# Splitting 1,408 of 2,048 weight columns on GpSimd, 640 on VectorE, in the unmixed up-projection groups

## The chip, the cores and the metric

One core of one Trainium2 chip runs the whole program. The metric is device time in microseconds (us); lower is better. The kernel before was timed three times, and one further execution was profiled.

## What is computed

Two layers of a hybrid decoder trunk, for 256 prompt positions and 8 sample rows (264 columns in all, T in the kernel). Each layer is a mixer (RWKV-7, HGRN2, spatial gating) and then a PEER layer: eight heads pick 16 of 16,384 single-neuron experts for each token.

```python
def peer_ffn(h, wq, keys, down, up):
    ...
        idx = e1 * PEER_N_KEYS + e2
        gate = jax.nn.softmax(sc.astype(jnp.float32), axis=-1)
        pre = jnp.einsum("td,thkd->thk", xt, down[idx])
        act = (jax.nn.gelu(pre.astype(jnp.float32), approximate=False) * gate).astype(xt.dtype)
        return jnp.einsum("thk,thkd->td", act, up[idx])
```

The kernel does not gather experts. It multiplies by all of `down` and all of `up`, and the gates of the experts that were not picked are zero. The change is in the product with `up`.

## The kernel before

`up` is read as 128 tiles of 128 experts x 1024 columns, in groups of two (GRP = 2). A half of the tiles is 32 groups (NGRP), so a layer has 64 groups, g = 0 to 63, and two layers have 128. Of the 64 groups of a layer the first 24 (MIXED) are interleaved on TensorE with two tiles of the down projection each; the other 40 follow one another with nothing between them. In this text the former are mixed groups and the latter unmixed ones.

fp32 precision is had from fp32r operands split in a high and a low part. For the weights of group g these steps run, over two buffers b = g % 2:

- SyncE (`up`, line 399): one 1 MB DMA into the raw tiles of `ring`; it waits until both low parts of group g - 2 are made (`ulo_done`, `alo_done`).
- ScalarE (`up_hi`, line 1222): waits for the DMA and until TensorE has finished group g - 2 (`out_mm`), which read the same buffer of UHL; then copies 2048 columns into the high part of UHL, and the activations into the high part of AHL.
- GpSimd (`up_lo`, line 1906): waits for the first of these copies (`uhi_done`) and subtracts the high part from the raw weights for the second tile of the pair, 1024 columns.
- VectorE (`low`, line 1827): waits for the second copy (`ahi_done`) and does the same for the first tile, 1024 columns, then for the activations (AHL, 528 columns).
- TensorE (`up`, line 913): waits for both low parts and runs 48 matmuls, 6 for each of 8 PSUM banks; after each bank it raises `out_mm`.
- VectorE (`gather`, line 1835): adds each finished bank to xT.

VectorE's order is written out in `group`: the first four banks of g are gathered, then `low` of g + 1 runs, in some groups a multiplication by second gates (`second_gated`), then the last four banks.

```python
                def group(g, turn, p=None):

                    gather(g, range(0, 4), turn)
                    low(g + 1, turn)
                    if p is not None:
                        second_gated(p, p % 4, turn)
                    gather(g, range(4, 8), turn)
```

All VectorE tensor-by-tensor operations are recorded under the helper's line 1356, ScalarE's copies under 983 and all matmuls here under 462, so the operations are told apart by their tiles.

Of the kernel before, what the change touches and what calls it, by code (L numbers as in the profile page):

```python
# [18 lines left out]
F32 = mybir.dt.float32  # L19
U32 = mybir.dt.uint32  # L20
BF16 = mybir.dt.bfloat16
ALU = mybir.AluOpType
# [4 lines left out]
D_MODEL = 1024  # L27
# [18 lines left out]
GRP = 2  # L46
# [6 lines left out]
EXTRA = 16  # L53
AHEAD = HALF + EXTRA
MIXED = (HALF - EXTRA) // GRP


PARS = [("mix_g", 8), ("ffn_g", 8), ("mu", RT), ("w0", 4), ("a0", 4), ("kk", 4), ("ka", 4), ("rk", 4),
# [51 lines left out]
def build(nc, d):  # L110
    ctx = ExitStack()
    with ctx:
        def sb(name, *shape, dt=F32):
            return ctx.enter_context(nc.sbuf_tensor(name, list(shape), dt))
# [4 lines left out]
        ring = sb("ring", P, 2 * RINGP, KD, P)  # L119
# [131 lines left out]
        UHL = sb("UHL", P, 2, 2, GRP, D_MODEL, dt=FR)  # L251
# [32 lines left out]
        def up_bank(g, k):  # L284

            return bank[2 + k % 4] if g < MIXED else bank[k]

# [3 lines left out]
        RAWD, RAWU = 6, 0  # L291
# [12 lines left out]
        S = {n: ctx.enter_context(nc.semaphore(n)) for n in dict.fromkeys(names)}  # L304
# [40 lines left out]
        def _(sp):  # L345
# [13 lines left out]
            for l in range(DEPTH):  # L359
# [39 lines left out]
                def up(g, slot, turn):  # L399

                    sp.wait_ge(S["ulo_done"], turn + (l * 2 * NGRP + g + 1))
                    sp.wait_ge(S["alo_done"], turn + (l * 2 * NGRP + g + 1))
                    sp.dma_start(ring[:, RAWU + 2 * slot:RAWU + 2 * slot + 2].rearrange("p s k m -> p s (k m)"),
                                 d["up"][l][:, bass.ds(turn * GRP + g * GRP, GRP)]).then_inc(up_in[slot], 16)
# [12 lines left out]
                def second_gates(r, buffer, turn):  # L417

                    sp.wait_ge(S["g1_out0"], (l + 1) * (NBLK + 1) // 2 * 16)
                    sp.wait_ge(S["g1_out1"], (l + 1) * (NBLK // 2) * 16)  # L420
                    sp.wait_ge(S["g1_mul"], turn * 2 + (l * NGRP + 2 * r + 2))
                    sp.dma_start(ING[buffer], DG[:, :, bass.ds(turn * 4 + r * 4, 4)].rearrange("k p e t -> p k e t"))\
                        .then_inc(S["g1_in"], 16)

                def mixed(g, turn, more=True):

                    up(g, g % 2, turn)
                    for c in range(2 * more):
                        down(AHEAD + 2 * g + 2 + c, (2 * g + 2 + c) % 4, turn * 2, -EXTRA)

                with sp.Fori(0, MIXED // 4 - 1) as i:
                    for r in range(2):
                        mixed(2 * r, i * 4)
                        mixed(2 * r + 1, i * 4)
                        second_gates(r, r, i * 2)
                for r in range(MIXED // 2 - 2, MIXED // 2):
                    mixed(2 * r, 0)
                    mixed(2 * r + 1, 0, 2 * r + 2 < MIXED)
                    second_gates(r, r % 2, 0)
                for g in range(MIXED, NGRP + 2):  # L440
                    up(g, g % 2, 0)
                    if g in (MIXED + 2, MIXED + 4):
                        r = (g - 2) // 2
# [894 lines left out]
        def _(dve):  # L1338
# [16 lines left out]
            def tt(out, a, b, op):  # L1355
                return dve.tensor_tensor(out, a, b, op)  # L1356
# [43 lines left out]
            for l in range(DEPTH):  # L1400
# [216 lines left out]
                for lev in range(1, LEV_H + 1):  # L1617
                    hx = HV[f"HX{lev % 2}"]
                    b = 1 << (lev - 1)
# [114 lines left out]
                for tc in range(3):  # L1734
                    m, nh = (P, PH) if tc < 2 else (64, 1)
# [32 lines left out]
                for tc in (2, 0, 1):  # L1768
                    m, nh = (P, PH) if tc < 2 else (64, 1)
# [11 lines left out]
                for tc in range(3):  # L1781
                    m = P if tc < 2 else DEC
# [44 lines left out]
                def low(g, turn):  # L1827

                    b = g % 2
                    dve.wait_ge(S["ahi_done"], turn + (l * 2 * NGRP + g + 1))  # L1830
                    tt(UHL[:, b, 1, 0], ring[:, RAWU + 2 * b].rearrange("p k m -> p (k m)"),
                       UHL[:, b, 0, 0].bitcast(F32), ALU.subtract)
                    tt(AHL[:, b, 1], ACTS[:, bass.ds(turn * GRP + g % NGRP * GRP, GRP), :], AHL[:, b, 0].bitcast(F32),
                       ALU.subtract).then_inc(S["alo_done"], 1)

# [7 lines left out]
# [8 lines that stand above are left out]
                need("g_evac", GB + (l + 1) * NB)  # L1851
                low(0, 0)
                group(0, 0)
                with dve.Fori(0, MIXED // 4 - 1) as i:
# [23 lines left out]
        @block.gpsimd  # L1878
        def _(pool):

            pool.sem_inc(S["dlo_done"], 4)
            pool.sem_inc(S["ulo_done"], 2)

            for l in range(DEPTH):

                for lev in range(1, LEV_H + 1):
                    for c in range(NHC):
                        pool.wait_ge(S["att_evac"], l * 2 * (LEV_H + 1) + 2 * lev + c + 1)
                        if lev > 1:
                            pool.wait_ge(S["at_add"], l * 2 * LEV_H + 2 * (lev - 2) + c + 1)  # L1890
                        pool.tensor_tensor(AT_[:, c], AT_[:, c], (T5, T6)[c], ALU.add).then_inc(S["at_add"], 1)  # L1891

                for n in range(2, 16):
                    s = QSLOTS[n // 2]
                    pool.wait_ge(S["dhi_done"], l * ND + n - 1)
                    pool.tensor_tensor(DHL[:, n % 2, 1], ring[:, 2 * s + n % 2].rearrange("p k m -> p (k m)"),  # L1896
                                       DHL[:, n % 2, 0].bitcast(F32), ALU.subtract).then_inc(S["dlo_done"], 1)
                    if n % 2:
                        pool.drain().then_inc(ring_free[s], 1)

                def down_lo(n, b, slot, turn):
                    pool.wait_ge(S["dhi_done"], turn + (l * ND + NQ + n + 1))
                    pool.tensor_tensor(DHL[:, b, 1], ring[:, RAWD + slot].rearrange("p k e -> p (k e)"),  # L1903
                                       DHL[:, b, 0].bitcast(F32), ALU.subtract).then_inc(S["dlo_done"], 1)

                def up_lo(g, b, turn):

                    pool.wait_ge(S["uhi_done"], turn + (l * 2 * NGRP + g + 1))
                    pool.tensor_tensor(UHL[:, b, 1, 1], ring[:, RAWU + 2 * b + 1].rearrange("p k m -> p (k m)"),  # L1909
                                       UHL[:, b, 0, 1].bitcast(F32), ALU.subtract).then_inc(S["ulo_done"], 1)  # L1910

                with pool.Fori(0, AHEAD // 4) as i:
                    for b in range(4):
                        down_lo(b, b % 2, b, i * 4)
                for b in range(2):
                    down_lo(AHEAD + b, b, b, 0)

                def mixed(g, turn):

                    up_lo(g + 1, (g + 1) % 2, turn)  # L1920
                    for c in range(2):
                        down_lo(AHEAD + 2 * g + 2 + c, c, (2 * g + 2 + c) % 4, turn * 2)

                up_lo(0, 0, 0)
                with pool.Fori(0, MIXED // 2 - 1) as i:
                    for b in range(2):
                        mixed(b, i * 2)
                mixed(MIXED - 2, 0)
                for g in (MIXED, MIXED + 1):
                    up_lo(g, g % 2, 0)  # L1930
                with pool.Fori(0, NGRP - MIXED // 2 - 1) as i:
                    for b in range(2):
                        up_lo(MIXED + 2 + b, b, i * 2)
# [94 lines left out]
```

## Time and profile before

| | before |
|---|---|
| median of 3 runs | 2968.42 us (2968.40 to 2971.78) |
| profiled execution, its own time | 2967.73 us |
| span of that execution's trace | 2965.8 us |
| PE busy | 2742.1 us, 92% |
| DVE (VectorE) busy | 1888.9 us, 64% |
| ACT (ScalarE) busy | 1127.9 us, 38% |
| POOL (GpSimd) busy | 1075.9 us, 36% |
| granted TensorE clock, mean | 0.975 |

The busy shares are averages over stages that differ. PE is the matmul engine, PEld its weight load, SP the queue of SyncE. The time of the profiled execution is 1.9 us longer than its span, which begins with the first and ends with the last instruction.

### The profile page before, as it was taken

How to read it: one execution, taken by the hardware profiler on the slowest of the kernel's cores; microseconds unless marked ns; L12 is line 12 of the kernel's file. 1: busy time of each engine (PE TensorE's matmuls, PEld its weight loads, DVE VectorE, ACT ScalarE, POOL GpSimd, SP SyncE). 2: the span in 40 equal slices, each digit the busy share in tenths (PEclk: the TensorE clock that was granted, in tenths of full speed). 3: DMA queues.
4: the chain of work that ended last, by engine and by line, in shares of the span. 5: the costliest groups of instructions: out<-in, count | busy, mean ns of one | idle time of the engine just before them, and what ended most of it. 6: DMA issues, size and time to landing. Idle time of an engine off the chain costs nothing.

```text
span 2965.8 us, 55557 instructions
## 1 busy us (share of the span) xinstructions
PE 2742.1 (92%) x20766; PEld 2529.3 (85%) x20766; DVE 1888.9 (64%) x3331; ACT 1127.9 (38%) x1682; POOL 1075.9 (36%) x444
## 2 busy tenths in 40 slices
PE   7899999989987999999988999999999889999997
PEld 5687777889987999999866877778999779999997
DVE  1663562299798554689817526533995975457887
ACT  1312320344487444333303124104445864443332
POOL 0000110478843656433300001004887245663332
PEclk9999999999999999999999999999999999999998
DMA  5222223255544566455452322233555446664543
GB/s 191 101 80 82 103 75 140 88 174 175 170 146 171 199 207 205 155 194 184 143 184 72 104 72 90 88 128 129 170 170 169 152 174 206 198 199 165 195 172 107
DMA packets 145453, 439.50 MB, mean 148 GB/s; under 512 B 62066, under 2 KB 63602, under 8 KB 126772
## 3 DMA queue, kind: packets, MB, share of 16 engines
q1 hardware_dynamic: 132548, 400.84, 39.7%
q10 hardware_dynamic: 12784, 37.00, 3.3%
q8 instruction: 82, 1.34, 0.2%
q14 instruction: 39, 0.32, 0.0%
HBM read 407.10 MB, written 30.15 MB: 147 GB/s over the span
## 4 chain that ended last, share of the span: by engine, by line
PE 61%; DVE 15%; issue 12%; POOL 8%; ACT 2%; DVEq 1%; DMA 0%; POOLq 0%; ACTq 0%; SPq 0%
PE banks L462 60%; POOL DHL L1903 7%; DVE arena L1356 3%; DVE OHE L1356 2%; DVE OHG L1356 2%; DVE ACTS L1356 1%; DVE AHL L1356 1%; ACT arena L983 1%; DVE UHL L1356 1%; POOL arena L1891 1%; DVE hT L1364 1%; DVE arena L1685 0%; DVE arena L1457 0%; DVEq L1356 0%; ACT L983 0%
## 5 line engine op out<-in xcount | busy, mean ns | idle before, releaser
L462 PE MATMUL banks<-HHL,DHL 128*128 128x264 f32 x6816 | 859.4, 287 | 23.6 <-POOL DHL L1903 12.1
L462 PEld LDWEIGHTS banks<-HHL,DHL 128*128 128x128 f32 x6816 | 844.2, 190 | 32.3 <-POOL DHL L1903 16.5
L462 PE MATMUL banks<-AHL,UHL 128*128 128x264 f32 x6144 | 773.3, 286 | 31.6 <-DVE AHL L1356 29.1
L462 PEld LDWEIGHTS banks<-AHL,UHL 128*128 128x128 f32 x6144 | 758.6, 189 | 41.9 <-issue 41.8
L1903 POOL TENSOR_TENSOR DHL<-ring,DHL 128x1024 fp32r<-128x1024 f32 x256 | 657.3, 2572 | 277.8 <-ACT DHL L983 276.0
L1356 DVE TENSOR_TENSOR xT<-xT,banks 128x264 f32<-128x264 f32 x1040 | 402.7, 423 | 388.8 <-PE banks L462 387.9
L462 PE MATMUL banks<-hT,ring 128*128 128x272 f32 (+1 forms) x2048 | 501.8, 403 | 9.7 <-issue 7.9
L1909 POOL TENSOR_TENSOR UHL<-ring,UHL 128x1024 fp32r<-128x1024 f32 x128 | 308.7, 2412 | 538.2 <-ACT UHL L983 538.2
L462 PEld LDWEIGHTS banks<-hT,ring 128*128 128x128 f32 x2048 | 394.4, 196 | 101.7 <-issue 23.1
L983 ACT ACTIVATE UHL<-ring 128x2048 fp32r<-128x2048 f32 x128 | 245.5, 1918 | 509.8 <-PE banks L462 486.7
L983 ACT ACTIVATE arena<-banks 128x264 f32<-128x264 f32 (+6 forms) x226 | 98.7, 455 | 635.9 <-PE banks L462 587.2
L983 ACT ACTIVATE DHL<-ring 128x1024 fp32r<-128x1024 f32 x284 | 298.6, 1052 | 102.2 <-PE banks L462 91.8
L1891 POOL TENSOR_TENSOR arena<-arena 128x512 f32<-128x512 f32 x28 | 39.8, 1437 | 756.8 <-DVE arena L1356 756.7
L1356 DVE TENSOR_TENSOR arena<-arena 128x512 f32<-128x512 f32 (+8 forms) x222 | 207.9, 957 | 145.0 <-ACT arena L983 139.8
L462 PEld LDWEIGHTS banks<-arena 64*64 64x64 f32 (+3 forms) x3376 | 196.4, 154 | 68.6 <-DVE arena L1356 35.3
L462 PE MATMUL banks<-arena 64*64 64x64 f32 (+7 forms) x3376 | 219.3, 244 | 35.6 <-DVE arena L1356 24.0
L1356 DVE TENSOR_TENSOR UHL<-ring,UHL 128x1024 fp32r<-128x1024 f32 x128 | 236.6, 1849 | 7.5 <-ACT AHL L983 7.5
L983 ACT ACTIVATE ACTS<-banks 128x264 f32 (+1 forms) x224 | 87.8, 392 | 288.8 <-PE banks L462 281.3
L462 PE MATMUL banks<-OHG,OH 128*128 128x128 f32 x1056 | 134.0, 282 | 46.0 <-DVE ACTS L1356 40.6
L1896 POOL TENSOR_TENSOR DHL<-ring,DHL 128x1024 fp32r<-128x1024 f32 x28 | 70.0, 2504 | 287.9 <-ACT DHL L983 287.9
L462 PEld LDWEIGHTS banks<-OHG,OH 128*128 128x128 f32 x1056 | 125.6, 195 | 53.1 <-issue 38.2
L462 PE MATMUL banks<-arena,ring 128*128 128x264 f32 x640 | 149.6, 392 | 11.5 <-DVE arena L1356 8.8
(118 smaller groups left out, 1925.1 us busy)
## 6 DMA issues: line engine op xcount, KB each, us to landing
ring<-down SPq DMA_DIRECT2D x256, 512.0 KB, 3.7
ring<-up SPq DMA_DIRECT2D x128, 1024.0 KB, 4.9
ring<-wm SPq DMA_DIRECT2D x100, 1024.0 KB, 5.0
hT<-second_gates SPq DMA_DIRECT2D x32, 528.0 KB, 4.9
second_gates<-ring ACTq DMA_DIRECT2D x12, 768.0 KB, 3.3
second_gates<-hT ACTq DMA_DIRECT2D x10, 768.0 KB, 3.3
ACTS<-extra_acts SPq DMA_DIRECT2D x2, 2112.0 KB, 9.8
arena<-hs ACTq DMA_DIRECT2D x2, 1280.0 KB, 6.1
```

The costliest lines, as they stand in the source:

```text
L462: return pe.matmul(out, lhsT, rhs, start=start, stop=stop)
L983: return act.activation(out, in_, fn, **kw)
L1356: return dve.tensor_tensor(out, a, b, op)
L1364: return dve.scalar_tensor_tensor(out=out, in0=a, scalar=s, in1=b, op0=op0, op1=op1)
L1891: pool.tensor_tensor(AT_[:, c], AT_[:, c], (T5, T6)[c], ALU.add).then_inc(S["at_add"], 1)
L1896: pool.tensor_tensor(DHL[:, n % 2, 1], ring[:, 2 * s + n % 2].rearrange("p k m -> p (k m)"), DHL[:, n % 2, 0].bitcast(F32), ALU.subtract). ...
L1903: pool.tensor_tensor(DHL[:, b, 1], ring[:, RAWD + slot].rearrange("p k e -> p (k e)"), DHL[:, b, 0].bitcast(F32), ALU.subtract).then_inc(S ...
L1909: pool.tensor_tensor(UHL[:, b, 1, 1], ring[:, RAWU + 2 * b + 1].rearrange("p k m -> p (k m)"), UHL[:, b, 0, 1].bitcast(F32), ALU.subtract) ...
```

## The change

A constant SHARE = 640 is added. In the unmixed groups (g from 24 on) VectorE's subtraction covers the first 640 columns of the first tile, and GpSimd's covers the other 384 columns of it and the 1024 of the second, 1408 in all, in one instruction. In the mixed groups both sizes stay at 1024. No instruction is added, removed or put in another place, and no wait changes. On GpSimd 40 instructions of a layer grow from 128x1024 to 128x1408, on VectorE 40 shrink from 128x1024 to 128x640.

```diff
+SHARE = 640
...
                     dve.wait_ge(S["ahi_done"], turn + (l * 2 * NGRP + g + 1))
-                    tt(UHL[:, b, 1, 0], ring[:, RAWU + 2 * b].rearrange("p k m -> p (k m)"),
-                       UHL[:, b, 0, 0].bitcast(F32), ALU.subtract)
+                    own = D_MODEL if g < MIXED else SHARE
+                    tt(UHL[:, b, 1, 0, 0:own], ring[:, RAWU + 2 * b].rearrange("p k m -> p (k m)")[:, 0:own],
+                       UHL[:, b, 0, 0, 0:own].bitcast(F32), ALU.subtract)
...
                     pool.wait_ge(S["uhi_done"], turn + (l * 2 * NGRP + g + 1))
-                    pool.tensor_tensor(UHL[:, b, 1, 1], ring[:, RAWU + 2 * b + 1].rearrange("p k m -> p (k m)"),
-                                       UHL[:, b, 0, 1].bitcast(F32), ALU.subtract).then_inc(S["ulo_done"], 1)
+                    rest = slice(D_MODEL if g < MIXED else SHARE, GRP * D_MODEL)
+                    pool.tensor_tensor(UHL[:, b, 1].rearrange("p j m -> p (j m)")[:, rest],
+                                       ring[:, RAWU + 2 * b:RAWU + 2 * b + 2].rearrange("p s k m -> p (s k m)")[:, rest],
+                                       UHL[:, b, 0].rearrange("p j m -> p (j m)")[:, rest].bitcast(F32), ALU.subtract)\
+                        .then_inc(S["ulo_done"], 1)
```

## Rows read from the trace of the kernel before

**Rows 1.** The page: span, and busy time of each engine.
```profile
span 2965.8 us, 55557 instructions
...
PE 2742.1 (92%) x20766; PEld 2529.3 (85%) x20766; DVE 1888.9 (64%) x3331; ACT 1127.9 (38%) x1682; POOL 1075.9 (36%) x444
```
**Rows 2.** Windows, layer 1: mixed groups, then unmixed; PE, PEld, DVE, ACT, POOL, clock, DMA.
```profile
2450.00:2680.00 230.00, 230.00 (x1890) 230.00 (x1890) 115.72 (x214) 100.46 (x119) 143.90 (x60) 1.00 0.60 196
2700.00:2945.00 245.00, 234.51 (x1872) 229.47 (x1872) 215.35 (x401) 94.31 (x77) 91.24 (x38) 1.00 0.49 174
```
**Rows 3.** Timeline, PE, mixed groups of layer 0: start, duration, instructions.
```profile
1208.35 6.00 PE L462 MATMUL banks<-AHL,UHL 128*128 128x264 f32 x48
1214.18 6.00 PE L462 MATMUL banks<-HHL,DHL 128*128 128x264 f32 x48
```
**Rows 4.** Timeline, PE, unmixed groups of layer 1; in brackets the idle time before.
```profile
2826.49 11.96 PE L462 MATMUL banks<-AHL,UHL 128*128 128x264 f32 x96 [1.15 <-DVE AHL L1356]
2838.96 11.96 PE L462 MATMUL banks<-AHL,UHL 128*128 128x264 f32 x96 [0.51 <-DVE AHL L1356]
2851.44 0.76 PE L462 MATMUL banks<-AHL,UHL 128*128 128x264 f32 x4 [0.51 <-DVE AHL L1356]
```
**Rows 5.** Waits in the unmixed stretch of layer 1: total us, times, longest.
```profile
PE banks L462 <- DVE AHL L1356: 9.6, 20, 1.1
```
**Rows 6.** Waits in the unmixed stretch of layer 0.
```profile
PE banks L462 <- DVE AHL L1356: 10.1, 19, 1.1
```
**Rows 7.** Timeline, layer 1, two groups: what ScalarE, GpSimd and VectorE do for UHL and AHL.
```profile
2838.57 1.91 ACT L983 ACTIVATE UHL<-ring 128x2048 fp32r<-128x2048 f32 x1 [3.38 <-PE banks L462]
...
2840.56 2.41 POOL L1909 TENSOR_TENSOR UHL<-ring,UHL 128x1024 fp32r<-128x1024 f32 x1 [3.43 <-ACT UHL L983]
...
2842.55 1.50 DVE L1356 TENSOR_TENSOR UHL<-ring,UHL 128x1024 fp32r<-128x1024 f32 x1
2843.97 0.70 DVE L1356 TENSOR_TENSOR AHL<-ACTS,AHL 128x528 fp32r<-128x528 f32 x1
...
2845.21 1.92 ACT L983 ACTIVATE UHL<-ring 128x2048 fp32r<-128x2048 f32 x1 [4.20 <-PE banks L462]
...
2847.21 2.40 POOL L1909 TENSOR_TENSOR UHL<-ring,UHL 128x1024 fp32r<-128x1024 f32 x1 [4.24 <-ACT UHL L983]
...
2848.39 2.30 DVE L1356 TENSOR_TENSOR UHL<-ring,UHL 128x1024 fp32r<-128x1024 f32 x1
2850.61 0.70 DVE L1356 TENSOR_TENSOR AHL<-ACTS,AHL 128x528 fp32r<-128x528 f32 x1
```
**Rows 8.** Timeline, layer 1: the longest overlap of a DVE and a POOL subtraction.
```profile
2822.26 2.40 POOL L1909 TENSOR_TENSOR UHL<-ring,UHL 128x1024 fp32r<-128x1024 f32 x1 [5.02 <-ACT UHL L983]
...
2822.81 2.93 DVE L1356 TENSOR_TENSOR UHL<-ring,UHL 128x1024 fp32r<-128x1024 f32 x1
```
**Rows 9.** Timeline, layer 0: a pair without overlap.
```profile
1360.56 2.40 POOL L1909 TENSOR_TENSOR UHL<-ring,UHL 128x1024 fp32r<-128x1024 f32 x1 [2.85 <-ACT UHL L983]
...
1363.12 1.22 DVE L1356 TENSOR_TENSOR UHL<-ring,UHL 128x1024 fp32r<-128x1024 f32 x1
```
**Rows 10.** Lines and tiles, whole trace: min/median/max ns of one.
```profile
L1909 POOL TENSOR_TENSOR UHL<-ring,UHL x128: 2387/2397/3337, 943.1 to 2934.5; 128x1024 fp32r<-128x1024 f32 x128
...
L1891 POOL TENSOR_TENSOR arena<-arena x28: 1262/1275/1779, 355.9 to 1865.9; 128x512 f32<-128x512 f32 x28
...
L1356 DVE TENSOR_TENSOR UHL<-ring,UHL x128: 1217/1735/2931, 943.6 to 2935.7; 128x1024 fp32r<-128x1024 f32 x128
...
L1356 DVE TENSOR_TENSOR AHL<-ACTS,AHL x128: 693/696/2839, 946.5 to 2937.9; 128x528 fp32r<-128x528 f32 x128
```
**Rows 11.** The page, costliest groups: busy us, mean ns, idle before.
```profile
L1891 POOL TENSOR_TENSOR arena<-arena 128x512 f32<-128x512 f32 x28 | 39.8, 1437 | 756.8 <-DVE arena L1356 756.7
```
**Rows 12.** The page, DMA issues: KB each, median us from issue to landing.
```profile
ring<-up SPq DMA_DIRECT2D x128, 1024.0 KB, 4.9
```

## The prediction

> **What bounds the kernel now.** I read the page first, then windows over the stage that the change touches, then its waits, then the timeline of two groups.
>
> On the page PE is busy for 92% of the span, VectorE for 64%, GpSimd for 36% [rows 1]. Read as an average this says that GpSimd has room for 384 more columns and that VectorE hardly matters. The windows say more. In the mixed groups PE is busy without a gap. In the unmixed ones it is busy for 234.51 of 245 us, and VectorE for 215.35, which is 88% [rows 2]. The clock is 1.00 in both, so it plays no part.
>
> What a group costs TensorE alone is the distance of two starts in the mixed stretch: 1214.18 - 1208.35 = 5.83 us for 48 matmuls; over several starts it is 5.84, or 11.68 us for two groups [rows 3]. Unmixed, PE starts at 2838.96 and again, after 96 matmuls, at 2851.44: 12.48 us for two groups [rows 4]. So two groups lose 0.80 us, and the wait in front of them is for VectorE's AHL, 20 times in one layer and 19 in the other [rows 5, 6]. There are 40 unmixed groups in a layer, 20 pairs; 40 pairs x 0.80 = 32 us is all that can be had in this stage.
>
> The timeline says who makes AHL late [rows 7]. The buffer of UHL that TensorE read in the group started at 2838.96 is refilled in this chain:
>
> - the group starts at 2838.96 and ScalarE's copy at 2845.21: 6.25 us, the group and a hand-over;
> - GpSimd starts 2.00 us later, at 2847.21, and takes 2.40, to 2849.61;
> - VectorE's UHL subtraction, begun at 2848.39, ends at 2850.69, which is 1.08 us after GpSimd's end;
> - AHL starts at 2850.61 (0.08 before that end; neighbours overlap so in the rows) and TensorE 0.83 us after that, at 2851.44.
>
> 6.25 + 2.00 + 2.40 + 1.08 - 0.08 + 0.83 = 12.48. The chain closes on itself after two groups, since there are two buffers, and its length is exactly what two groups take. The other buffer's chain has the same links: AHL at 2843.97 plus 0.83 is 2844.80, just when TensorE's previous group is through (2838.96 + 5.84).
>
> The important link is the third. VectorE's subtraction takes 1.50 us, 2.30 us or 2.93 us for the same 1024 columns, and each time it ends 1.08 us after GpSimd's: 2840.56 + 2.41 = 2842.97 against 2844.05; 2849.61 against 2850.69 [rows 7]; 2824.66 against 2825.74 [rows 8]. Where GpSimd had ended before (1362.96) it takes 1.22 from its own start at 1363.12 [rows 9]. So it makes no headway while GpSimd's subtraction runs, and after that it needs its whole time but 0.14. GpSimd's own duration is the same 2.40 with and without overlap. **GpSimd and VectorE thus stand in series in this chain**, not side by side; the busy share of GpSimd hides that.
>
> The Trainium skill says the same of the cause (SBUF — State Buffer, Who interferes with whom): a VectorE instruction with two SBUF inputs and a GpSimd instruction that reads SBUF take one shared read interface in turns, for a whole instruction. By that rule the trace agrees, with the 1.08 us above. A reader of another page (Advanced Engine Details and Errata, Mode Summary) finds a note that names only VectorE's two-port modes as blocked; by that note these fp32 subtractions would run side by side, and the change would come out as the first rival below. The rows decide against it.
>
> **The change, part by part.**
>
> *VectorE, 384 columns fewer.* Slope between AHL at 528 columns, 693 ns, and UHL undisturbed at 1024, 1217 ns: 524 / 496 = 1.056 ns a column [rows 10], so 384 x 1.056 = 0.41 us off the link of 1.08, which becomes 0.67. In proportion to the whole instruction it would be 1217 x 384 / 1024 = 0.46. I take 0.41, since a fixed part does not shrink.
>
> *GpSimd, 384 columns more.* No subtraction of 1408 columns is in the trace. Between 512 columns (median 1275) and 1024 (2397) the slope is 2.19 ns, so +0.84 us and a duration of 3.24 [rows 10]. Lower end: with the mean of the 512-column row, 1437 [rows 11], the slope is 1.875, +0.72. Upper end: in proportion, 2397 / 1024 = 2.34, +0.90. I take 0.84, because both medians are of instructions that ran undisturbed.
>
> *The loop.* 0.84 longer and 0.41 shorter, both in series: +0.43 us, from 12.48 to 12.91 for two groups. GpSimd is slower per column by a factor of two, and moving columns to it costs the difference. Times 20 loops in each of two layers: 40 x 0.43 = **17.4 us**, unrounded. Lower end: 0.72 - 0.46 = 0.26, 10.6 us. Upper end: 0.90 - 0.41 = 0.49, 19.7 us.
>
> The skill prices a 2048-column fp32 add on GpSimd at 4497 ns (GPSIMD Engine Reference, Elementwise — side-by-side cycle accounting), 2.20 ns a column in proportion; by that the 1024 columns here would take 2.25 us where the row has 2.40. With 384 x 2.20 the sum would be 17.5 us, estimated; with the page's 3.09 us for 1408 columns set against the row's 2.40, it would be 11 us.
>
> *Parts that cost nothing.* GpSimd's `ulo_done` comes later by 0.84, at about 8.25 + 3.24 = 11.49 into the loop; TensorE waits for it, but AHL follows it by more than a microsecond, so it never is the last. The next 1 MB transfer waits for both low parts; AHL is the last of the two before and after. It lands 4.9 us after its issue [rows 12], and ScalarE wants it 6 us after it; this cover grows. VectorE's gathers after `low` are pushed as far as TensorE is. What VectorE does in the time gained is wait behind GpSimd. The first unmixed group of a layer is different: its GpSimd part is over long before, so VectorE's 0.41 is a true saving, at most 0.8 us for both layers, and probably lost in the next loop; I take 0. The mixed groups, the down projection and both mixers are untouched.
>
> Against the profiled execution, 2967.73 + 17.4 = 2985.1. The median of the runs is 0.7 above that execution, so the forecast of the median is **2985.8 us**.
>
> **Rivals.**
>
> *They run side by side after all (faster).* If VectorE's subtraction were not held, it would start 3.59 us after the group (2842.55 against 2838.96) and be over long before GpSimd; the loop would be 6.25 + 2.00 + 3.24 + about 0.15 = 11.64, just under the 11.68 that TensorE needs. All of the stage's loss would go: -32 us, 2936. The point that decides is whether VectorE ends 0.67 after GpSimd or before it. Against it stand rows 7 and 8. A partial form, in which GpSimd's longer instruction can be entered in its middle, has nothing for it. Chance 0.03.
>
> *GpSimd's extra columns are cheap (no change).* If the 384 columns cost it 0.41 us or less, the loop keeps its length, 2968. That needs 1.06 ns a column, half of any slope between its rows. Or the loop has slack that I overlooked; but the sum of its links is its period to 0.01 us. Chance 0.04.
>
> *The order of the two flips (slower than forecast).* If GpSimd starts later than 3.59 us into a group, VectorE takes its turn first and GpSimd's 3.24 us come after it: 3.59 + 0.81 + 3.24 = 7.64 against 5.84, a loss of 1.8 us for that group. It needs a ScalarE copy that is late by over a microsecond, by a transfer or by the gates' multiplication; the nearest in this stretch is GpSimd 0.55 before VectorE [rows 8]. If it happened in 5 to 10 groups, 9 to 18 us would come on top: 2995 to 3004. Against it: transfers get more time, not less. Chance 0.06.
>
> **How the numbers follow.** Forecast 0.87, no change 0.04, faster 0.03, slower still 0.06. The forecast's own range is 2979 (10.6) to 2988 (19.7). For the half-understood irregular places (a few in a layer where the wait was already longer, 1.15 us in one [rows 4]) I allow 4 us below, and up to 2994 towards the third rival: 2975 to 2994. A change of 0.2%, 5.9 us, is about what can be told from none; the forecast's whole range is above that. Faster 0.03, same 0.05, slower 0.92.
>
> **What would show it.** In the profile of the changed kernel: GpSimd's 128x1408 rows at 3.2 us (2.9 to 3.3); VectorE's 128x640 rows ending 0.67 us after GpSimd's, mostly 1.1 to 3 us long from their start, so that VectorE's busy time for UHL falls little or rises; two groups every 12.9 us on PE; the wait of PE for AHL near 20 x 0.9 us a layer instead of 9.6; mixed groups at 5.84 as before. The forecast is wrong if a 128x640 row ends before the GpSimd row beside it, if PE's last wait turns to UHL from GpSimd or to a transfer, or if the pairs come at 12.5 us or less.

## The result, and the profile after

| | before | changed |
|---|---|---|
| median | 2969.02 us (6 runs, 2962.9 to 2971.8) | 2988.49 us (6 runs, 2981.8 to 2998.3) |
| ratio to before | 1 | 1.0071, 95% interval 1.0057 to 1.0085 |
| profiled execution, its own time | 2967.73 us | 2991.29 us |

The kernel became slower by 19.5 us. The page of the changed kernel, span and busy times (they answer to [rows 1]):

```profile
span 2988.8 us, 55557 instructions
PE 2746.7 (92%) x20766; PEld 2532.6 (85%) x20766; DVE 1903.9 (64%) x3331; ACT 1128.0 (38%) x1682; POOL 1141.0 (38%) x444
```

VectorE has 40 x 2 x 384 columns less to subtract and is busy for 15 us **more**. In such rows waiting for GpSimd counts as busy. The groups by shape (whole trace; us busy, mean ns), and from the timeline of layer 1 a row of VectorE with no GpSimd row beside it:

```profile
L1912 POOL TENSOR_TENSOR UHL<-ring,UHL 128x1408 fp32r<-128x1408 f32 x80 | 258.4, 3230 | 274.3 <-ACT UHL L984 274.3
...
L1357 DVE TENSOR_TENSOR UHL<-ring,UHL 128x640 fp32r<-128x640 f32 x80 | 167.0, 2088 | 0.0
```

```profile
2706.06 0.82 DVE L1357 TENSOR_TENSOR UHL<-ring,UHL 128x640 fp32r<-128x640 f32 x1
```

GpSimd's 1408 columns take 3.23 us. VectorE's 640 columns need 0.82 us undisturbed, but the mean row is 2.09 us long: most of it is waiting. Windows of layer 1, mixed groups and then the unmixed stretch (columns as in [rows 2]):

```profile
2450.00:2680.00 230.00, 230.00 (x1891) 230.00 (x1890) 116.28 (x216) 101.80 (x120) 141.34 (x59) 1.00 0.61 206
2708.90:2968.80 259.90, 240.10 (x1920) 235.10 (x1918) 228.41 (x408) 96.57 (x79) 126.04 (x39) 1.00 0.47 170
```

Mixed groups run without a gap, as before. Timeline of PE in the unmixed groups, where [rows 4] had 12.48 us between starts:

```profile
2859.63 11.96 PE L463 MATMUL banks<-AHL,UHL 128*128 128x264 f32 x96 [0.95 <-DVE AHL L1357]
2872.54 11.96 PE L463 MATMUL banks<-AHL,UHL 128*128 128x264 f32 x96 [0.95 <-DVE AHL L1357]
2885.44 11.96 PE L463 MATMUL banks<-AHL,UHL 128*128 128x264 f32 x96 [0.94 <-DVE AHL L1357]
```

The starts are 12.90 us apart, and the gap in front, 0.51 before, is 0.95. The wait for AHL in the unmixed stretch of layer 1 (total, times, longest), against [rows 5]:

```profile
PE banks L463 <- DVE AHL L1357: 18.1, 19, 1.7
```

And the chain itself, against [rows 7]: the timeline of ScalarE, GpSimd and VectorE for UHL and AHL.

```profile
2865.88 1.92 ACT L984 ACTIVATE UHL<-ring 128x2048 fp32r<-128x2048 f32 x1 [4.63 <-PE banks L463]
...
2867.88 3.23 POOL L1912 TENSOR_TENSOR UHL<-ring,UHL 128x1408 fp32r<-128x1408 f32 x1 [3.85 <-ACT UHL L984]
...
2869.06 2.73 DVE L1357 TENSOR_TENSOR UHL<-ring,UHL 128x640 fp32r<-128x640 f32 x1
...
2871.71 0.69 DVE L1357 TENSOR_TENSOR AHL<-ACTS,AHL 128x528 fp32r<-128x528 f32 x1
```

Read link by link: the group's start at 2859.63 to ScalarE at 2865.88 is 6.25 us, then 2.00 to GpSimd, 3.23 to its end at 2871.11, 0.68 to VectorE's end at 2871.79, AHL from 2871.71, and 0.83 from there to PE at 2872.54. Only the third and fourth link differ from before: +0.83 and -0.40.

What the stage cost in all I take from the timeline, from the end of the last matmul of the down projection to the end of the last one with AHL, in both layers: before 257.72 and 257.34 us, changed 265.97 and 266.25. That is **+17.2 us**. The stage holds 41 products with `up` in each layer, since that of the last mixed group follows the last of the down projection; at 5.84 us each TensorE alone would need 2 x 239.4 = 478.9 us, so the kernel before loses 36 us here. The profiled executions differ by 23.6 us. Of the other 6.4 us, 4.8 lie ahead of this stage in layer 0, 2.2 between the two stages, -1.2 behind them and 0.6 outside the span; the change touches none of these (see the last section).

### The profile page after: what moved, and what is told of

It is laid out like the page before. It is cut to its first block, busy times and chain, and to the rows that moved or that the text cites. A ratio compares the mean times of both kernels' runs of the same rounds, so it can differ in the third digit from the quotient of the medians.

```text
span 2988.8 us, 55557 instructions
## 1 busy us (share of the span) xinstructions
PE 2746.7 (92%) x20766; PEld 2532.6 (85%) x20766; DVE 1903.9 (64%) x3331; ACT 1128.0 (38%) x1682; POOL 1141.0 (38%) x444
## 4 chain that ended last, share of the span: by engine, by line
PE 61%; DVE 14%; issue 13%; POOL 8%; ACT 2%; DVEq 1%; DMA 1%; POOLq 0%; ACTq 0%; SPq 0%
PE banks L463 60%; POOL DHL L1905 7%; DVE arena L1357 3%; DVE OHE L1357 2%; DVE OHG L1357 2%; DVE ACTS L1357 1%; DVE AHL L1357 1%; POOL arena L1893 1%; ACT arena L984 1%; DVE UHL L1357 1%; DVE arena L1686 0%; DVE arena L1458 0%; DVEq L1357 0%; DVE OH L1357 0%; DVE hT L1365 0%
## 5 line engine op out<-in xcount | busy, mean ns | idle before, releaser
L1912 POOL TENSOR_TENSOR UHL<-ring,UHL 128x1408 fp32r<-128x1408 f32 (+1 forms) x128 | 375.1, 2932 | 490.5 <-ACT UHL L984 490.5
L1357 DVE TENSOR_TENSOR UHL<-ring,UHL 128x640 fp32r<-128x640 f32 (+1 forms) x128 | 251.5, 1965 | 7.5 <-ACT AHL L984 7.5
```

The source lines that it names most:

```text
L1912: pool.tensor_tensor(UHL[:, b, 1].rearrange("p j m -> p (j m)")[:, rest], ring[:, RAWU + 2 * b:RAWU + 2 * b + 2].rearrange("p s k m -> p ( ...
```

## The experiments

Seven kernels were run, each compared with runs of the kernel before: median 2968.6 of 15 runs for VectorE's part alone, 1280, 1408 and the copy in two, 2969.4 of 17 runs for the other three. "Stage" is the sum over both layers, measured as above, good to 0.1 us; before it is 515.0 us. Line numbers differ by a few between kernels.

### VectorE's part alone

```diff
-                    rest = slice(D_MODEL if g < MIXED else SHARE, GRP * D_MODEL)
+                    rest = slice(D_MODEL, GRP * D_MODEL)
```

GpSimd is back at 1024 columns, VectorE has 640; 384 columns of the low part are made by nobody.

> VectorE's part of the change alone: 640 columns on VectorE, 1024 on GpSimd; the low parts of columns 640 to 1023 of the first tile are left out. Series theory: the two-group loop loses 0.41 us, 12.48 to 12.07 us, VectorE ends 0.67 us after GpSimd instead of 1.08, and the time falls by 40 x 0.41 = 16 us against before. Rival (VectorE only stands in GpSimd's shadow, its columns are free): no change. Rival (the two run side by side): minus 32 us.

Measured: 2955.43 us, ratio 0.9958 (0.9943 to 0.9973), 13 us faster where 16 were expected; stage 500.6, minus 14.4. The timeline has two groups in 12.08 us (GpSimd's starts at 2859.01 and 2871.09), and VectorE's 640 columns end 0.67 or 0.68 us after GpSimd:

```profile
2859.01 2.41 POOL L1912 TENSOR_TENSOR UHL<-ring,UHL 128x1024 fp32r<-128x1024 f32 x1 [3.43 <-ACT UHL L984]
...
2860.59 1.51 DVE L1357 TENSOR_TENSOR UHL<-ring,UHL 128x640 fp32r<-128x640 f32 x1
...
2865.25 2.40 POOL L1912 TENSOR_TENSOR UHL<-ring,UHL 128x1024 fp32r<-128x1024 f32 x1 [3.83 <-ACT UHL L984]
...
2866.44 1.89 DVE L1357 TENSOR_TENSOR UHL<-ring,UHL 128x640 fp32r<-128x640 f32 x1
```

VectorE's columns are on the path, both rivals fall. The other half of the change comes from the difference of the stages (532.2 in the changed kernel): 532.2 - 500.6 = 31.6 us for 384 more columns on GpSimd, where the sum had 40 x 0.84 = 33.6.

### The share turned the other way

```diff
-SHARE = 640
+SHARE = 1280
...
-                    tt(UHL[:, b, 1, 0, 0:own], ring[:, RAWU + 2 * b].rearrange("p k m -> p (k m)")[:, 0:own],
-                       UHL[:, b, 0, 0, 0:own].bitcast(F32), ALU.subtract)
+                    tt(UHL[:, b, 1].rearrange("p j m -> p (j m)")[:, 0:own],
+                       ring[:, RAWU + 2 * b:RAWU + 2 * b + 2].rearrange("p s k m -> p (s k m)")[:, 0:own],
+                       UHL[:, b, 0].rearrange("p j m -> p (j m)")[:, 0:own].bitcast(F32), ALU.subtract)
```

> The change's direction turned round: VectorE 1280 columns, GpSimd 768. Series theory: GpSimd 2.40 - 256 x 0.00219 = 1.84 us, VectorE's remainder 1.08 + 256 x 0.001056 = 1.35; the loop is 12.48 - 0.56 + 0.27 = 12.19 us, so 40 x 0.29 = 12 us faster than before. The chain of one group (3.59 to the subtraction, 1.49, then 0.75 to TensorE) is 5.83, just under 5.84. Rival (the change hurt for a reason of its form, one instruction across two tiles, not for its size): slower than before by a few us.

Measured: 2959.06 us, ratio 0.9974 (0.9962 to 0.9985); stage 506.0, minus 9.0. PE starts are 12.18 us apart:

```profile
2853.94 11.96 PE L463 MATMUL banks<-AHL,UHL 128*128 128x264 f32 x96 [0.22 <-DVE AHL L1357]
2866.12 11.96 PE L463 MATMUL banks<-AHL,UHL 128*128 128x264 f32 x96 [0.22 <-DVE AHL L1357]
```

The form, one instruction over two tiles, does not hurt on VectorE: the time falls. On GpSimd it is settled further down, where each of two instructions stays within one tile and the stage is as long as in the changed kernel.

The same with SHARE = 1408:

> VectorE 1408 columns, GpSimd 640: the mirror of the change. Series theory: GpSimd 1.56 us, remainder 1.49, loop 12.48 - 0.84 + 0.41 = 12.05 us; the chain of one group over VectorE alone is 3.59 + 1.62 + 0.75 = 5.96, or 11.93 for two, just below. 40 x 0.43 = 17 us faster than before. Rival (VectorE's own chain binds more than its rows say): no faster than with 1280 columns.

Measured: 2955.57 us, ratio 0.9956 (0.9940 to 0.9972); stage 501.5, minus 13.5. GpSimd's starts are 12.05 us apart, as worked out:

```profile
2858.44 1.57 POOL L1913 TENSOR_TENSOR UHL<-ring,UHL 128x640 fp32r<-128x640 f32 x1 [4.55 <-ACT UHL L984]
...
2870.49 1.56 POOL L1913 TENSOR_TENSOR UHL<-ring,UHL 128x640 fp32r<-128x640 f32 x1 [4.57 <-ACT UHL L984]
```

In the regular loop the two steps of this size mirror each other, +0.42 and -0.43 us. Over the stage 384 columns one way cost 17.2 us and the other way gave 13.5; where the rest went is said in the section on the prediction.

And with SHARE = 1536:

> VectorE 1536 columns, GpSimd 512. The two-buffer loop would be 12.48 + 512 x (0.001056 - 0.00219) = 11.90 us, but VectorE's chain within one group is now 3.59 + 1.76 + 0.75 = 6.10 us, 12.20 for two, and binds. Theory: slower than with 1408 columns, 12.20 against 12.05 us, 40 x 0.15 = 6 us; about 11 us faster than before. Rival (only the loop over GpSimd counts): 23 us faster than before.

Measured: 2956.89 us, ratio 0.9955 (0.9939 to 0.9971); stage 504.0, minus 11.0. The rival's 23 us did not come. In the regular groups VectorE no longer meets GpSimd, and its own period is the bound (timeline):

```profile
2862.34 1.29 POOL L1913 TENSOR_TENSOR UHL<-ring,UHL 128x512 fp32r<-128x512 f32 x1 [4.76 <-ACT UHL L984]
...
2863.78 1.75 DVE L1357 TENSOR_TENSOR UHL<-ring,UHL 128x1536 fp32r<-128x1536 f32 x1
...
2869.85 1.75 DVE L1357 TENSOR_TENSOR UHL<-ring,UHL 128x1536 fp32r<-128x1536 f32 x1
```

One group takes 2869.85 - 2863.78 = 6.07 us, where 6.10 was expected. The stage says that 1536 is 2.5 us worse than 1408; the medians, 1.3 us apart and measured on two chips, do not tell them apart. So the turn is near 1408, but these runs do not fix it.

### ScalarE's copy in two, GpSimd's columns first

```diff
-                    f(UHL[:, b, 0].rearrange("p a m -> p (a m)"),
-                      ring[:, RAWU + 2 * b:RAWU + 2 * b + 2].rearrange("p s k m -> p (s k m)"), ACT.Copy)\
-                        .then_inc(S["uhi_done"], 1)
+                    cut = 0 if g < MIXED else min(SHARE, D_MODEL)
+                    raw = ring[:, RAWU + 2 * b:RAWU + 2 * b + 2].rearrange("p s k m -> p (s k m)")
+                    hi = UHL[:, b, 0].rearrange("p a m -> p (a m)")
+                    f(hi[:, cut:], raw[:, cut:], ACT.Copy).then_inc(S["uhi_done"], 1)
+                    if cut:
+                        f(hi[:, 0:cut], raw[:, 0:cut], ACT.Copy)
```

With SHARE = 1024, the sizes of before:

> Shares as before (1024 and 1024), but in the unmixed groups ScalarE's copy of 2048 columns is two copies of 1024, GpSimd's tile first, so that GpSimd starts after 1.05 us instead of 1.92. Loop theory: the link of 2.00 becomes about 1.13 and the loop 11.61 us, under the 11.68 that TensorE needs; nearly the whole loss goes, minus 30 us, about 2938. Rival (the wait is set by VectorE's and GpSimd's work, not by when GpSimd starts): no change. Rival (transfer next in line: it lands just before ScalarE asks): part of the gain stays out, and ScalarE's wait for it grows.

Measured: **2939.09 us**, ratio 0.9912 (0.9895 to 0.9928), 29.5 us faster than before; stage 489.2, minus 25.8. The timeline: GpSimd starts 1.14 us after ScalarE instead of 2.00,

```profile
2864.47 2.01 ACT L984 ACTIVATE UHL<-ring 128x1024 fp32r<-128x1024 f32 x2 [3.29 <-PE banks L463]
2865.61 2.42 POOL L1915 TENSOR_TENSOR UHL<-ring,UHL 128x1024 fp32r<-128x1024 f32 x1 [3.44 <-ACT UHL L984]
...
2867.68 1.44 DVE L1360 TENSOR_TENSOR UHL<-ring,UHL 128x1024 fp32r<-128x1024 f32 x1
```

and PE runs 912 matmuls, 19 groups, without a gap:

```profile
2790.22 11.96 PE L463 MATMUL banks<-AHL,UHL 128*128 128x264 f32 x96 [0.26 <-DVE AHL L1360]
2804.05 113.00 PE L463 MATMUL banks<-AHL,UHL 128*128 128x264 f32 x912 [1.86 <-DVE AHL L1360]
```

GpSimd's subtraction is as long as before, and VectorE's ends 1.09 us after it, as before; its rows are shorter only by waiting. The point at which GpSimd may start moved, and 25.8 of the 36 us that the stage loses went: it is the loop that binds, until TensorE does. The regular groups now come at 11.71 us for two, next to TensorE's 11.68. What stays are four or five waits in a layer. The one of 1.86 us is behind a transfer: issued at 2791.26, just after one of second gates, it landed at 2798.50, 7.24 us later, and ScalarE's copy began at 2798.68. It has a second price. After this wait 14 matmuls come 0.22 us apart instead of 0.12, with a granted clock of 0.56 from 2804.05 to 2807.50, where 1.2 GHz was granted for most of the window. The group took 7.48 us, 1.6 more than its 5.84. No other wait in the unmixed groups of the nine profiles was followed by such a stretch, not even one of 2.49 us in the last experiment below.

The same with the change's shares, 640 and 1408:

> The change's shares (640 and 1408) with ScalarE's copy split in the unmixed groups: GpSimd's 1408 columns first, VectorE's 640 second. Loop theory: the first copy takes about 1.38 us instead of 1.92, so the link of 2.00 becomes 1.46 and the loop of the changed kernel, 12.90, becomes 12.36 us: 40 x 0.54 = 22 us off the changed kernel, about 2967, 5 us under before and some 27 above the split with equal shares. Rival (the split alone does the work, the share no longer matters once it is there): as fast as the split with 1024 and 1024, 2939.

Measured: 2965.62 us, ratio 0.9993 (0.9983 to 1.0003); stage 511.6. PE starts are 12.37 us apart (12.36 expected):

```profile
2835.81 11.96 PE L463 MATMUL banks<-AHL,UHL 128*128 128x264 f32 x96 [0.41 <-DVE AHL L1360]
2848.18 11.96 PE L463 MATMUL banks<-AHL,UHL 128*128 128x264 f32 x96 [0.41 <-DVE AHL L1360]
```

Against the changed kernel the stage is 20.6 us shorter, against the split with equal shares 22.4 us longer, where 27 were expected. The share still has its price while the loop is longer than TensorE's 11.68 us.

### GpSimd's 1408 columns in two instructions

```diff
+                    for part in (slice(D_MODEL, 2 * D_MODEL), slice(SHARE, D_MODEL))[0:1 if g < MIXED else 2]:
+                        ins = pool.tensor_tensor(UHL[:, b, 1].rearrange("p j m -> p (j m)")[:, part],
...
+                    ins.then_inc(S["ulo_done"], 1)
```

> The change's shares, but GpSimd's 1408 columns are two instructions, 1024 and then 384. Theory (turns are taken by whole instructions): VectorE's subtraction, already waiting, goes in between and ends about 0.68 us after the first GpSimd row, not after the second; the second then stands before or beside AHL. It costs 0.15 us more of fixed time; the loop is 12.9 to 13.1 us, so as slow as the changed kernel or a few us slower. Rival (GpSimd keeps its turn as long as it has work): VectorE ends 0.68 after the second row, and the loop is 13.05 us, plus 6.

Measured: 2984.70 us, ratio 1.0058 (1.0042 to 1.0075); stage 533.3, 1.1 more than the changed kernel. This excess is one place of layer 0, where a copy waited for a transfer and PE then waited 2.49 us; elsewhere the stage is about 1 us shorter. The timeline shows the turns; the row of 3.96 us holds both GpSimd instructions, the last row is the second of them alone.

```profile
2862.21 3.96 POOL L1913 TENSOR_TENSOR UHL<-ring,UHL 128x1024 fp32r<-128x1024 f32 x2 [3.68 <-ACT UHL L984]
...
2863.52 1.77 DVE L1357 TENSOR_TENSOR UHL<-ring,UHL 128x640 fp32r<-128x640 f32 x1
2865.22 1.52 DVE L1357 TENSOR_TENSOR AHL<-ACTS,AHL 128x528 fp32r<-128x528 f32 x1
```

```profile
2864.57 1.60 POOL L1913 TENSOR_TENSOR UHL<-ring,UHL 128x384 fp32r<-128x384 f32 x1
```

GpSimd's second row starts at 2864.57, about where the first ends. VectorE, waiting since 2863.52, goes in between and ends at 2865.29, 0.7 us after that. GpSimd's 384 columns now wait and end at 2866.17, 0.88 us after VectorE's end. VectorE's AHL, issued at 2865.22, waits for them in turn and ends at 2866.74, 0.57 us after theirs; alone it takes 0.69. So a turn is one instruction, whoever waits gets the next, and cutting the work into more turns does not shorten the sum. These rows show the turns; what the two engines share is not tested by a run.

## Why the prediction was right

Forecast 2985.8 us, measured 2988.5, +19.5 against a forecast +17.4.

*What bounds.* The loop of two groups over ScalarE, GpSimd, VectorE and TensorE, 12.48 us, against 11.68 that TensorE needs. The copy in two showed it directly: with one link shortened by 0.86 us the loop fell to 11.71 us, and of some 20 gaps on PE in a layer four or five were left. With 1408 and 1280 columns on VectorE the period came out as 12.05 and 12.18 us where the links sum to 12.05 and 12.19.

*GpSimd, +0.84 us, duration 3.24.* Measured 3.23. The slope from the 512-column row held up to 1408 columns; the upper end, in proportion, would have been 3.30, the lower 3.12.

*VectorE, -0.41 us, remainder 0.67.* Measured 0.68, and alone 12.08 us a loop for 12.07.

*The loop, 12.91 us, +17.4 us.* Measured 12.90, and the stage +17.2. The count of 40 loops is right for the regular groups only. VectorE's part alone gave 14.4 us of the stage where 40 loops have 16.4, 1280 columns 9.0 for 11.6, and 1408 columns 13.5 for 17. The start of each group, compared with the kernel before, shows where the rest is: every regular loop has nearly its full amount, and it is the first groups of a layer and the two places where ScalarE's copy waits for a transfer or the second gates that give less, or at times more. Around the second of these, in layer 1, VectorE's part alone lost 0.20 us in a loop instead of gaining 0.41, and 1408 columns lost 0.64. That the change comes so near to its sum is partly luck: 20 loops are 8.6 us, layer 0 has 8.3 and layer 1 8.9.

*Parts at nothing.* The mixed groups stayed at full speed. The first unmixed group behaved as said: TensorE began it 0.40 us earlier, and the next loop took that back, +0.83 instead of +0.43. `ulo_done` did not become the last wait; the wait in front of PE is AHL in 19 cases of a layer, 16.9 and 18.1 us, and one of 1.67 us at the start is put down to a gather. Transfers held ScalarE's copy in five groups, against three before, so their cover did not grow everywhere.

*The rivals.* Side by side: refuted by the rows, and by the two GpSimd instructions, between which VectorE waits its turn. Cheap extra columns: no, 2.16 us per thousand. The flip of order did not occur in the unmixed groups; where both were at work GpSimd came 0.48 us or more ahead of VectorE even at the irregular places. What it does to GpSimd can be read at the first groups of a layer, here layer 0 of the kernel before; the row of GpSimd holds two instructions, of which the second begins at 945.41:

```profile
943.07 5.68 POOL L1909 TENSOR_TENSOR UHL<-ring,UHL 128x1024 fp32r<-128x1024 f32 x2 [21.30 <-ACT UHL L983]
...
943.63 2.92 DVE L1356 TENSOR_TENSOR UHL<-ring,UHL 128x1024 fp32r<-128x1024 f32 x1 [3.73 <-ACT AHL L983]
```

VectorE's row ends at 946.55. GpSimd's second one ends at 948.75, 2.20 us after that, and is 3.34 us long, the maximum in [rows 10]. The prediction passes over it where it calls GpSimd's duration the same with and without overlap: GpSimd waits too, when it comes second.

*What the sum did not have.* About 2 us of the median, and 6.4 us of the profiled pair, lie outside the stage. The last section is on that. The interval of the ratio, 16.9 to 25.2 us, holds the 17.2 us of the stage, so nothing more has to be explained by the change.

## What to carry to other kernels

Where two engines take turns, an instruction each, their times add on the path, so splitting work between them gains nothing by overlap; each column should go to whichever is faster per column until that engine's own chain binds. Engines with 36% or 64% busy shares can both be critical: follow one buffer around until it returns, sum the links, and compare with what the bounding engine needs. Then look for the cheapest link to shorten; here that was not the subtraction but the point at which GpSimd was allowed to begin, and a copy cut in two gave 25.8 us of the stage where the best share gave 13.5.

## What the runs showed that I had not expected

The spread between executions of one kernel, up to 16 us, is as large as the effects. In three profiles the code ahead of the unmixed groups is the same, yet the last down projection of layer 0 ends at 1220.2 us before, at 1225.0 in the changed kernel and at 1217.2 with 1408 columns on VectorE. Windows from 300 to 400 us (columns as in [rows 2]; the clock is the third number from the right), first the kernel before, then the changed one, then 1408 columns:

```profile
300.00:400.00 100.00, 91.64 (x531) 77.21 (x529) 57.31 (x79) 34.33 (x68) 19.82 (x14) 0.92 0.26 90
```

```profile
300.00:400.00 100.00, 94.22 (x507) 79.31 (x507) 55.77 (x76) 34.49 (x67) 17.52 (x12) 0.86 0.26 90
```

```profile
300.00:400.00 100.00, 91.36 (x561) 78.22 (x561) 58.73 (x81) 36.09 (x71) 19.85 (x14) 0.98 0.26 90
```

The granted clock in this stretch of the first mixer, where TensorE is busy for 91 to 94 of 100 us, was 0.92, 0.86 and 0.98 of full speed, and the matmuls done in it 531, 507 and 561. The order of the three is that of the stage's start. The other six profiles do not keep it: VectorE's part alone had 0.95 here and ended the last down projection of layer 0 at 1224.0, the copy in two had 0.98 and ended it at 1220.4. Over the first 900 us the order holds better: the three kernels that came last (1224.0 to 1226.4) have the lowest mean clocks, 0.960 to 0.968, and the six others (1217.2 to 1220.6) have 0.970 to 0.975. That one follows from the other is what these rows suggest, not what a run has shown. It means that a step of a few microseconds is better read from the stage's own rows than from whole runs.

Also unexpected: GpSimd's rows, which I took to be rough, were regular to some 10 ns: means of 1296, 1571, 1850 and 3230 ns for 512, 640, 768 and 1408 columns, which is 2.16 ns a column and 0.19 us besides.
